# Second stack's up projections as products over token halves, with the taps on ScalarE

## The reference, cut to what matters

```python
def causal_depthwise_conv(x, w):          # w: 3 taps
    xp = jnp.pad(x, ((0, 0), (K - 1, 0), (0, 0)))
    y = xp[:, 0:S, :] * w[0]
    for tap in range(1, K):
        y = y + xp[:, tap:tap + S, :] * w[tap]
    return y

def conv_ffn(xn, w_up, conv_w, conv_b, w_down):
    h = causal_depthwise_conv(xn @ w_up, conv_w) + conv_b
    g, u = jnp.split(h, 2, axis=-1)
    return (jax.nn.gelu(g) * u) @ w_down
```

## Time and profile before

| what | value |
| --- | --- |
| median of 3 runs (lowest, highest) | 2711.86 us (2708.48, 2712.26) |
| span of the profiled execution | 2704.1 us |
| PE busy | 2665.1 us, 99% |
| DVE busy | 1624.6 us, 60% |
| ACT busy | 495.6 us, 18% |
| POOL busy | 160.6 us, 6% |
| granted PE clock, mean | 0.997 |
| DMA | 458.78 MB, mean 170 GB/s |

### The profile page before, as it was taken

One profiled execution on the slowest core, in us unless ns is written; L12 is line 12 of the kernel. 1 busy time (PEld: TensorE's weight loads), 2 busy tenths in 40 slices (PEclk: granted clock), 3 DMA queues, 4 the chain that ended last, 5 costly groups with the idle time before them and its releaser, 6 DMA issues.

```text
span 2704.1 us, 40392 instructions
## 1 busy us (share of the span) xinstructions
PE 2665.1 (99%) x16636; PEld 2426.1 (90%) x16636; DVE 1624.6 (60%) x3372; ACT 495.6 (18%) x869; POOL 160.6 (6%) x138
## 2 busy tenths in 40 slices
PE   9999999999999999999999999999999999999998
PEld 8899899788999999889878899988889998888998
DVE  4587665655677778675564666535347762324876
ACT  2011343421100100243431100013210011211000
POOL 0000000000330330000000231000000000000000
PEclk9999999999999999999999999999999999999999
DMA  9887421526446556531244444442334444343442
GB/s 379 313 332 259 149 94 63 197 106 227 164 172 229 192 224 221 211 141 63 87 172 157 177 171 172 156 171 95 139 121 160 156 158 168 119 153 112 156 156 94
DMA packets 74440, 458.78 MB, mean 170 GB/s; under 512 B 8308, under 2 KB 9216, under 8 KB 28176
## 3 DMA queue, kind: packets, MB, share of 16 engines
q1 hardware_dynamic: 73120, 449.34, 45.7%
q0 software_dynamic: 1136, 6.86, 0.7%
HBM read 455.08 MB, written 1.09 MB: 169 GB/s over the span
## 4 chain that ended last, share of the span: by engine, by line
PE 91%; DVE 5%; DMA 2%; DVEq 1%; ACT 1%; issue 1%; ACTq 0%
PE psum L531 20%; PE psum L749 14%; PE psum L691 14%; PE psum L598 9%; PE psum L915 8%; PE psum L797 4%; PE psum L986 3%; PE psum L574 2%; PE psum L704 2%; PE psum L935 2%; PE psum L620 2%; PE psum L862 2%; DMA aring<-astream 1%; PE psum L809 1%; PE psum L633 1%; PE psum L888 1%
## 5 line engine op out<-in xcount | busy, mean ns | idle before, releaser
L531 PE MATMUL psum<-h,ring 128*128 128x256 f32 x1568 | 341.7, 379 | 1.4 <-DVE arena L1785 0.8
L531 PEld LDWEIGHTS psum<-h,ring 128*128 128x128 f32 x1568 | 297.4, 190 | 43.2 <-DVE arena L1785 1.1
L749 PE MATMUL psum<-arena 128*128 128x128 f32 x2112 | 249.7, 275 | 0.3 <-DVE arena L1685 0.3
L749 PEld LDWEIGHTS psum<-arena 128*128 128x128 f32 x2112 | 242.6, 192 | 0.5 <-DVE arena L1685 0.5
L598 PE MATMUL psum<-aring,ring 128*128 128x256 f32 x1088 | 237.3, 379 | 1.7 <-issue 1.7
L915 PE MATMUL psum<-h,ring 128*128 128x256 f32 x1024 | 235.7, 383 | 0.0
L598 PEld LDWEIGHTS psum<-aring,ring 128*128 128x128 f32 x1088 | 205.8, 190 | 29.9 <-issue 2.4
L915 PEld LDWEIGHTS psum<-h,ring 128*128 128x128 f32 x1024 | 192.7, 193 | 26.2 <-issue 1.9
L749 PE MATMUL psum<-arena,ring 128*128 128x128 f32 x1584 | 191.6, 275 | 0.0
L749 PEld LDWEIGHTS psum<-arena,ring 128*128 128x128 f32 x1584 | 184.3, 192 | 0.2
L691 PE MATMUL psum<-arena 128*128 128x128 f32 x1440 | 170.6, 275 | 0.0
(11 more groups left out here) (449 smaller groups left out, 3874.2 us busy)
## 6 DMA issues: line engine op xcount, KB each, us to landing
ring<-wstream SPq DMA_DIRECT2D x349, 1024.0 KB, 4.8
aring<-astream SPq DMA_DIRECT2D x128, 512.0 KB, 4.8
arena<-astream SPq DMA_DIRECT2D x16, 512.0 KB, 18.2
arena<-wstream SPq DMA_DIRECT2D x3, 1024.0 KB, 20.5
arena<-decays POOLq DMA_DIRECT2D x2, 1024.0 KB, 5.2
sq<-decays POOLq DMA_DIRECT2D x2, 1024.0 KB, 4.9
kst<-const SPq DMA_DIRECT2D x1, 1280.5 KB, 8.9
x<-xT SPq DMA_DIRECT2D x1, 1024.0 KB, 4.9
```

The lines of the kernel that those rows point to most:

```text
L531: mm = pe.matmul(out, lhsT=tile_at(at[0] % RING, t), rhs=rhs(k), start=k == 0, stop=k == kt - 1)
L749: mm = pe.matmul(out, lhsT=w, rhs=v, start=m == 0 and name in ("M1", "M5", "M3", "M4"), stop=m == NF // 2 - 1, skip_group_check=True)
```

## The change

The up projections of the second stack run slabs 0 to 2 plain and slabs 3 to 21 as seven products, in both layers.

- DVE multiplies the operands by the root first (`h` from `h2`, two instructions of 128 x 1024) and makes `up_tokens` from them; PE waits for this (`conv_tokens`) ahead of slab 3. The three plain slabs still use `h2` and are scaled on the way out of PSUM.
- PSUM banks: slab s uses the pair 2 * (s % 4), so four slabs can be open.
- POOL makes two of the four weight sums of each slab (`conv_weight_sums`) when PE has finished slab s - 2; DVE makes the other two (`other_weight_sums`).
- The evacuation writes straight into the padded buffers `convs` (two of them), with one copy and four additions for a seven-product slab.
- The three taps move to ACT: six Identity activations a slab with the tap as scale, into `conv_terms`. DVE adds the three terms (`convolved`, two additions of 128 x 512), one slab later; the Gelu stays on ACT; the product with the gate (`gate`) comes two slabs later.
- `cbuf` becomes part of a larger buffer `cvb`, whose memset on POOL and use in `keep_running` follow.

```diff
-CONV_QUICK = (4, 7, 10, 13, 16)
+CONV_PLAIN = 3
...
+        cbuf = cvb[:, P:].rearrange("p (a t) -> p a t", a=2)
+        convs = [cbuf, area(25680, 2, T + 3)]
+        u2_c11 = [cvb[:, 0:2 * (P + 3)].rearrange("p (a t) -> p a t", a=2)[:, :, 0:P],
+                  area(21000, 2, 2600)[:, :, 2083:2083 + P]]
...
+        conv_acc = [gate4[:, 2 * b:2 * b + 2] for b in range(2)]
+        taps_even = sq[:].rearrange("p (j a) t -> p j (a t)", a=2)
+        conv_terms = [[taps_even[:, j] for j in range(3)],
+                      [aring[:, 2, 0:2 * T], aring[:, 2, 2 * T:4 * T], condb[:, 0:2 * T]]]
...
+            def conv_weight_sums(layer, s):
+                first = DEPTH * SLABS_1 + (layer + 1) * (SLABS_2 // 2) - 33
+                i = first + s
+                w = ring[:, i % RING].rearrange("p (a t) -> p a t", a=4)
+                new = up_sums[:, s % 2].rearrange("p a u t -> p a (u t)")
+                pool.wait_ge(landed[i % RING], landing(i))
+                pool.wait_ge(slab_used, first + (1 if s < CONV_PLAIN + 2 else s - 1))
+                nc.gpsimd.tensor_tensor(new[:, 0], w[:, 2], w[:, 3], ALU.add)
+                nc.gpsimd.tensor_tensor(new[:, 1], w[:, 0], w[:, 2], ALU.subtract).then_inc(conv_first_sums, 1)
...
+                for s in range(CONV_PLAIN, NF):
+                    conv_weight_sums(layer, s)
...
-                    if s >= 3:
-                        pe.wait_ge(bank_free, cnt.value("bank_free", s - 2))
-                    elif s == 0:
+                    if s == 0:
                         fresh()
-                    if s in CONV_QUICK:
-                        if CONV_QUICK.index(s):
-                            pe.wait_ge(bank_free, cnt.value("bank_free", CONV_QUICK[CONV_QUICK.index(s) - 1] + 1))
-                        nth = len(CONV_QUICK) * layer + CONV_QUICK.index(s) + 1
-                        mm = block_products(slot, up_sums[:, nth % 2], 4, rhs, lambda: pe.wait_ge(conv_sums, nth))
+                    elif s >= CONV_PLAIN + 1:
+                        pe.wait_ge(bank_free, cnt.value("bank_free", {4: 2, 5: 3, 6: 3}.get(s, s - 3)))
+                    if s >= CONV_PLAIN:
+                        if s == CONV_PLAIN:
+                            pe.wait_ge(conv_tokens, layer + 1)
+                        nth = 2 * ((NF - CONV_PLAIN) * layer + s - CONV_PLAIN)
+                        mm = block_products(slot, up_sums[:, s % 2], 2 * (s % 4), scaled,
+                                            dict(M6=nth + 1, M3=nth + 2))
...
-            def gelu_gates(layer):
-                a = C2["cb"][0]
-                for s in range(NF):
-                    act.wait_ge(inputs_for_act, cnt.next("inputs_for_act"))
-                    E(gate4[:, 0], gate4[:, 0], ACT.Gelu_apprx_tanh, bias=p2[:, layer, a + s:a + s + 1]
-                      ).then_inc(functions_for_dve, 1)
+            def conv_gates(layer):
+                def par(name, off):
+                    a = C2[name][0] + off
+                    return p2[:, layer, a:a + 1]
+                for s in range(NF + 1):
+                    if s < NF:
+                        act.wait_ge(inputs_for_act, cnt.next("inputs_for_act"))
+                        for j in range(3):
+                            for a in range(2):
+                                bias = dict(bias=par("cb", 22 + s)) if j == 0 and a == 1 else {}
+                                last = E(conv_terms[s % 2][j][:, a * T:(a + 1) * T],
+                                         convs[s % 2][:, a, 1 + j:1 + j + T], ACT.Identity,
+                                         scale=par("cw", 44 * j + 22 * a + s), **bias)
+                        last.then_inc(functions_for_dve, 1)
+                    if s >= 1:
+                        act.wait_ge(inputs_for_act, cnt.next("inputs_for_act"))
+                        g = conv_acc[(s - 1) % 2][:, 0]
+                        E(g, g, ACT.Gelu_apprx_tanh, bias=par("cb", s - 1)).then_inc(functions_for_dve, 1)
...
+                first_conv = DEPTH * SLABS_1 + (layer + 1) * (SLABS_2 // 2) - 33
+                def terms_ready(s):
+                    dve.wait_ge(functions_for_dve, base + max(1, 2 * s))
+                def gate_ready(s):
+                    dve.wait_ge(functions_for_dve, base + min(2 * s + 3, 2 * NF))
+                def evacuate(s):
+                    dve.wait_ge(slab_used, cnt.next("slab_used"))
+                    dst = convs[s % 2]
+                    if s < CONV_PLAIN:
+                        TT(dst[:, :, 3:], psum[:, s].rearrange("p (a t) -> p a t", a=2), both(std[:]), ALU.mult
+                           ).then_inc(bank_free, 1)
+                    else:
+                        low = psum[:, 2 * (s % 4)]
+                        high = psum[:, 2 * (s % 4) + 1].rearrange("p (a t) -> p a t", a=4)
+                        u2, u43, m1 = u2_c11[s % 2][:, 0:1], quads[:, 1:3], quads[:, 3:4]
+                        V.tensor_copy(quads[:, 3], low[:, 0:P])
+                        D()
+                        TT(u2_c11[s % 2], m1.broadcast_to((P, 2, P)), low[:, P:3 * P].rearrange("p (a t) -> p a t", a=2),
+                           ALU.add)
+                        D()
+                        TT(u43, u2.broadcast_to((P, 2, P)), high[:, 1:3], ALU.add)
+                        D()
+                        TT(dst[:, :, 3 + P:], u43, high[:, 0:2], ALU.add)
+                        TT(dst[:, 1, 3:3 + P], quads[:, 2], low[:, 3 * P:], ALU.subtract).then_inc(bank_free, 1)
+                    D().then_inc(inputs_for_act, 1)
+                def gate(s):
+                    gate_ready(s)
+                    v = conv_acc[s % 2]
+                    TT(hidden[:, s], v[:, 1], v[:, 0], ALU.mult)
+                    if s % 4 == 3:
+                        D()
+                        token_sums(hidden, down_tokens, s // 2 - 1, 2)
+                    if s == NF - 1:
+                        D()
+                        token_sums(hidden, down_tokens, s // 2, 1).then_inc(weights_summed, 1)
+                def convolved(s):
+                    terms_ready(s)
+                    v, t = flat(conv_acc[s % 2]), conv_terms[s % 2]
+                    TT(v, t[0], t[1], ALU.add)
+                    D()
+                    TT(v, v, t[2], ALU.add).then_inc(inputs_for_act, 1)
+                V.memset(convs[1][:, :, 0:3], 0.0)
+                def other_weight_sums(s):
+                    w = ring[:, (first_conv + s) % RING].rearrange("p (a t) -> p a t", a=4)
+                    new = up_sums[:, s % 2].rearrange("p a u t -> p a (u t)")
+                    dve.wait_ge(conv_first_sums, (NF - CONV_PLAIN) * layer + s - CONV_PLAIN + 1)
+                    TT(new[:, 2], new[:, 0], w[:, 0], ALU.subtract).then_inc(conv_sums, 1)
+                    D()
+                    TT(new[:, 3], w[:, 1], new[:, 2], ALU.subtract).then_inc(conv_sums, 1)
                 root_of_mean(KD * P)
-                first = DEPTH * SLABS_1 + (layer + 1) * (SLABS_2 // 2) - 33
-                def sums_ahead(q):
-                    i = first + q
-                    w = ring[:, i % RING].rearrange("p (a t) -> p a t", a=4)
-                    nth = len(CONV_QUICK) * layer + CONV_QUICK.index(q) + 1
-                    new = up_sums[:, nth % 2].rearrange("p a u t -> p a (u t)")
-                    dve.wait_ge(landed[i % RING], landing(i))
-                    TT(new[:, 0], w[:, 2], w[:, 3], ALU.add)
-                    TT(new[:, 1], w[:, 0], w[:, 2], ALU.subtract)
-                    D()
-                    TT(new[:, 2], new[:, 0], w[:, 0], ALU.subtract)
-                    D()
-                    TT(new[:, 3], w[:, 1], new[:, 2], ALU.subtract).then_inc(conv_sums, 1)
-                for s in range(NF):
-                    dve.wait_ge(slab_used, cnt.next("slab_used"))
-                    if s in CONV_QUICK:
-                        pb = psum[:, 5].rearrange("p (a t) -> p a t", a=4)
-                        add_products(8, psum[:, 4], pb[:, 0:2], pb[:, 1:3], lambda: None)
-                        TT(quads[:, 10], quads[:, 2], psum[:, 4, 3 * P:], ALU.subtract).then_inc(bank_free, 1)
+                base = cnt.value("functions_for_dve")
+                for a in range(0, KD, 4):
+                    TT(h[:, a:a + 4], h2[:, a:a + 4], both(std[:], 4), ALU.mult)
+                D()
+                token_sums(h, up_tokens, 0, 4).then_inc(conv_tokens, 1)
+                for s in range(NF + 2):
+                    if s < NF:
+                        evacuate(s)
+                    if s >= 2:
+                        gate(s - 2)
+                    if 1 <= s <= NF:
+                        convolved(s - 1)
+                    if CONV_PLAIN <= s + 2 < NF:
                         D()
-                        TT(cbuf[:, :, 3:3 + T], quads[:, 8:12].rearrange("p (a u) t -> p a (u t)", a=2), both(std[:]),
-                           ALU.mult)
-                    else:
```

(34 more changed lines are left out.)

14 lines of the change are left out of this document (8 added, 6 removed).

## The result

The changed kernel takes 2721.54 us (median of 5 runs, 2715.60 to 2724.74) against 2711.35 (2708.48 to 2712.26) for the kernel before in the same rounds. The ratio is 1.0037, with a 95% interval from 1.0026 to 1.0048, so it is 10.2 us slower. The forecast was 23 us slower.

A forecast was written before the change was run, and what follows sets the result against it. PE was taken as the bound, busy 2665.1 of 2704.1 us. Waits of 20.7 us less 9.2 gain make 11.5 us a layer, 23 for both; with the median's 7.8 above the span, 2735 us, range 2694 to 2752.

The forecast's parts named there:

- PE's gain: Second stack's up projections: 14 more seven-product slabs a layer, 0.66 us each, 18.4 us over two layers if nobody is late.
- A meeting: Up slabs: a POOL sum and a DVE addition with both operands in SBUF take turns, costing DVE 0.89 us each.
- DVE keeps up: Rival for the up slabs: PE loses only the tail, 1.5 us a layer; 2696 us, faster; chance 16%.
- slab 3: First seven-product slab: PE waits for a weight sum behind root, scalings, token sums, evacuations and ACT's taps; 2 us a layer.
- slabs 10 to 19: Up slabs where PE goes at DVE's pace, each four taking 30 us instead of 25; 14 us of waits a layer.
- slabs 20 and 21: Last up slabs: PE waits, with the down slabs' weight sums at DVE's iteration 18; 3 us a layer.
- tail (down slabs 1 and 2): Start of the down projection: the last gate and token sum end later behind slab 21; 1.7 us a layer.
- From here the lateness grows until PE waits: Up slabs after the second token sums: both POOL sums fall among DVE's additions, 7.2 us an iteration; allowance used up near slab 10.
- I take 7 to 8 of them: Meetings in four up slabs once PE waits, from a possible 4 to 8; gives 30 us, 7.5 us a slab.
- one a slab: Rival: only one meeting a slab, since PE's wait shifts POOL's start; 6.8 us a slab, 2706 to 2720 us; chance 20%.
- the ends of the sum: One meeting a slab: 3 us a layer slower, 2718 us; every POOL sum met at 1.0 us: 17 us, 2746.
- 0.05 us moves a layer by 4 us: DVE's work in up slabs: 0.05 us less in each slab delays the first wait and moves a layer by 4 us.

The follow-up runs named there:

- e1: Changed kernel with POOL's two weight sums of slabs 3 to 21 left out, so two of four weight sums hold old data; 2694.32 us.
- e2: Changed kernel with POOL's two weight sums replaced by two memsets into the same place, which read nothing from SBUF; 2694.22 us.
- e10: Changed kernel with POOL's sums released by DVE's progress and POOL making two of four weight sums of the first two down slabs; 2696.92 us.
- e9: Changed kernel with ten unused 128x128 products on PE ahead of M6 in slabs 11 and 19; 2723.46 us.
- e8: Changed kernel with one more DVE drain behind each evacuation, 0.07 to 0.08 us a slab; 2724.89 us.
- after: The changed kernel itself, without any experiment's edit, against the kernel before; 2721.54 us, ratio 1.0037.
- e3: Changed kernel, whole computation, with POOL also waiting until DVE has ended the weight sums of the slab before; 2699.09 us, and 2699.92 in a second set.
- e5: Changed kernel, whole computation, with all four weight sums made on DVE and none on POOL; 2729.70 us.

## Why the prediction was right in direction and too high in size

**Right.** PE's gain is 6.91 to 6.25 us where nobody is late. DVE's work by itself was put at 5.39 us and stands at 5.39 in the timeline. A meeting costs 0.90 (0.89 was forecast), and POOL's sums are over 1.4 us. The reading that in the rest of the first stack the two never meet was too strong: at the start of each of the three projections they meet as well (three DVE instructions of 1.49 to 1.50 us, at 1520.45, 1521.87 and 1528.75 in the last one). It changes no term of the sum. DVE keeps up until about slab 10: the first wait in the middle stands at slab 11, then at 15, 19 and 21, all released by DVE's weight sum. e1 and e2 show that the meetings cause all waits in the up slabs but 0.08 and 0.43 us at slab 21; the tail of 1.5 us a layer comes without them. The rival "DVE keeps up" had its time right: 2696 forecast for next to no meetings, 2694.3 measured in e1, without any, and 2696.9 in e10, with those of the gate's product left.

**The terms of the sum**, in us for a layer (first, last), measured as what slabs take above 6.25:

| term | forecast | measured |
| --- | --- | --- |
| slab 3 | 2 | 0.93, 0.94 |
| slabs 10 to 19 | 14 | 10.8, 9.5 |
| slabs 20 and 21 | 3 | 1.55, 1.83 |
| tail (down slabs 1 and 2) | 1.7 | 1.54, 1.54 |
| waits together | 20.7 | 14.8, 13.9 |
| less PE's gain | 9.2 | 9.2 |
| slower by | 11.5 | 5.6, 4.7 |

**The step that failed** is "From here the lateness grows until PE waits", with its "I take 7 to 8 of them". In four slabs there are 5 meetings with DVE's additions, not 7 or 8: two in the iteration behind the token sums, one in each of the other three (from M6 of slab 11 to that of 15, and again on to that of 19, in the first layer). From M6 to M6 the four slabs take 2106.22 - 2078.18 = 28.04 us, and the forecast's own terms give it with 5: 4 x 5.39 + 1.9 + 5 x 0.9 = 28.0, 7.0 us a slab instead of 7.5. The reason is the one that the rival "one a slab" had named: a wait of PE moves its slab end, and with it POOL's next start, back beside DVE's PSUM part. The timeline shows it (POOL's idle time of 6.26 us in place of 2.87). How far back it moves is a near thing, though: in e9's last layer POOL came some 0.3 us earlier against DVE, and three slabs with two meetings each followed at 7.18 us. I had walked through the steps up to the first wait and carried the last state on, instead of walking on through one wait. The truth lies between the forecast and this rival, whose 2706 to 2720 us end just below the 2721.5 measured.

The same error stands in the ends of the sum. e8 lengthened each slab by some 0.075 us and moved the layers by 0.6 and 1.7 us, where "0.05 us moves a layer by 4 us" would have made it 6. Lateness that is paid off by PE's wait and by POOL's shift doesn't add up.

**Slab 3** has the right place and twice the size. The meetings at the root were there as forecast, three instructions lengthened to 1.33 to 1.45 us, but ACT's six taps were too dear. Six were priced at 6 x 0.51 = 3.1 us, and these are slab 0's six and the load of the Gelu's table:

```profile
2020.13 2.59 ACT L1525 ACTIVATE sq<-cvb,p 128x256 f32<-128x256 f32 x6 [10.32 <-DVEq L2419]
...
2025.23 1.28 ACT L1532 ACT_TABLE_LOAD   x1
```

That is 0.43 each, since queued ones overlap; a duration of a lone instruction was taken for a pace. In a row on DVE I had taken off that overlap, on ACT not. The 1.4 us that the sum gave less these 0.5 are the 0.9 measured; the rest of the 2 was an allowance for the table load, which stands behind the weight sum that PE waited for (L2447, done at 2025.01) and cost PE nothing here. The Trainium skill (ScalarE: Activation LUTs, What ACT_TABLE_LOAD costs) has activations in a row overlap by some 93 ns each, and the record of the six agrees with it: 6 x 0.51 less 5 x 0.093 is 2.6 us.

**Slabs 20 and 21** were put at 3 us and cost 1.55 and 1.83. Two meetings with the down slab's weight sums are in it (L1721 and L1723, 1.76 and 1.58 us at 2141.06 and 2142.91); without POOL's sums 0.08 and 0.43 are left (e1). Which part of the 3 us was too dear no run shows. **The tail** was right, and so was its cause, since it stands in e1 too: 0.88 + 0.66 us against 1.7.

**What stays open.** The 4.9 us ahead of 600 us in the one profiled execution, and where the 0.3 us come from that make it two meetings a slab in the last layer of e9 and one in after. What the last 1.3 us wait of e10 would take to go was not tried.

## What to carry to other kernels

If work is given to POOL beside a busy DVE (81% here), first sort DVE's instructions into those with a PSUM operand and those with two SBUF inputs, and release POOL by DVE's own progress, so that its reads fall beside the first kind: the same sums on the same engine then made 2699 us instead of 2722. When lateness is forecast, walk on through the first wait of the bound engine, since everything that starts from that engine shifts with it: it is the pattern behind the wait that repeats. And give the range both patterns where they lie close: here 0.3 us parted one meeting a slab from two. Where one engine sets the pace, what another wins in its waits (here the clock) is waited off again.

## What the hardware showed that was not expected

- **Turns depend on what POOL reads.** A POOL sum with SBUF inputs lengthens DVE's SBUF addition from 0.69 to 1.59 us, and a memset of 0.95 us at the same place leaves it at 0.69 (e2). The gate's product of 128x256 went from 0.42 to 0.93 us beside a sum (e3), and a DVE instruction with a PSUM operand kept its 0.28 or 0.42 in every kernel.
- **PE's clock behind waits.** In after, three of the five waits of 2.7 us and more (2.75, 2.85 and 3.21 us) were followed by 5 us at a granted clock of 0.66, a mean of time at 1.2 and at 2.4 GHz. The 24 records behind them took 4.3 to 4.54 us instead of 2.94. Behind the other two, of 2.83 and 2.76 us, it stayed at 1.00. Ten products in the wait kept 1.00 behind it. The length of the wait alone doesn't tell: in e5 the clock fell behind five of the ten waits of 1.8 to 2.3 us as well, each time one of 2.07 or 2.08 (0.57 over 2079 to 2083 us), and its slab 11 took 10.22 us.
- **The fall cost next to nothing.** Slab 11 of the last layer took 1.6 us longer by it and slab 15 then had no wait, and keeping the clock up at slabs 11 and 19 won nothing (2721.5 us in after, 2723.5 in e9).
